# Bidirectional gated linear attention: from tiles of 66 keys to tiles of 128 keys and one of 16

## The chip, the cores and the metric

One core of a Trainium2 chip runs the whole program. The metric is the device time of one execution in microseconds (us). The core has a matmul engine (PE, with its weight loads shown as PEld), a vector engine (DVE), a scalar engine (ACT), GpSimd (POOL) and SyncE (SP), which here issues most DMAs.

## The reference

The program computes two transformer blocks one after the other on 512 tokens of width 1024. The change lies in the first block, in the mixer. 16 meta tokens stand before the 512, so there are T = 528. Of one projection it takes a differential softmax attention (4 heads) and a gated linear attention (GLA, 4 heads with 64 key and 128 value channels) that runs in both directions:

```python
def step(state, inp):                      # chunks of 64 tokens, one direction
    qc, kc, vc, gc = inp
    b = jnp.cumsum(gc, axis=2)
    rel = b[:, :, :, None, :] - b[:, :, None, :, :]
    decay = jnp.exp(jnp.where(mask, rel, -jnp.inf))
    attn = jnp.einsum('bhid,bhjd,bhijd->bhij', qc, kc, decay)
    o = jnp.einsum('bhij,bhjv->bhiv', attn, vc) + jnp.einsum('bhid,bhdv->bhiv', qc * jnp.exp(b), state)
...
    return (o_f + o_b)[:, pad:]
```

The output of the meta tokens is dropped after the mixer. After it come a router over 128x128 expert keys with 16384 small experts, and the second block (its modulation vectors come from a 1024x6144 matrix, the "ada" weights, that depends on nothing in the first block).

## The kernel before

The work is written by hand for each engine as a sequence of stages; semaphores with fixed counts join them. In the mixer the order is: norm, projections (z, gates, gla_qk, gla_v), linear attention, softmax attention, output projection.

**The linear attention has no state.** The sum of the log gates over tokens (`decay_sum`) is scanned once for each direction. Every pair (key, query) lies in one block of a binary tree over the tokens, at the level where they part. For each level and direction, a unit of work (`exponent` on POOL, `decays` on ACT and DVE) makes an array `decayed`: keys and queries times the exponential of their distance from the middle of that block. Scores of a pair are then a plain product over 64 channels, with no pair of tokens multiplied by a large number. Tokens are cut in NJ = 8 tiles of JT = 66 keys; levels have half blocks of 264, 132, 66 and 33 tokens, and leaves of 33 tokens have arrays of their own.

**Jobs and slots.** Two heads (a pair a) are done together, their 64 channels on partitions 0 to 63 and 64 to 127, their scores in PSUM banks 0 and 1. A pair has 12 jobs, each with up to 512 columns of scores of 66 keys. `scores(n)` of the PE program makes them; ACT (head 0 of the pair, first 8 jobs) and DVE (all else, and all that take a mask) copy them to SBUF as weights `residual`; `applying(n)` multiplies with the values (`gla_v`) and adds to bank 4 + h. The last four jobs hold the 66x66 blocks on the diagonal four times over: next to the leaves forward and backward and the 33-token level in both directions, each with its mask. So there are 24 slots.

**Fill.** Between `scores(n)` and `applying(n)` the PE does other work listed in `MIX_FILL[n]`: tiles of the projections gla_r, da_q, da_k, da_v (each 24 bf16 matmuls in `columns_tile` or `rows_tile`: high and low halves of an f32 product), rotations (`rope`), and "ada" blocks g = 0 to 6. An ada block (`modulation`) is 16 f32 matmul passes with 32 output rows over a 2 MB block of weights straight from its DMA stage; the next call first turns the former row (L651). Blocks 7 to 11 go with steps 0 to 4 of the softmax attention, one each, in PSUM bank 7, which they share with the sums for the head norms (L641).

**Weights** come through two f32 stage buffers (`STAGES = 2`), three high and three low ones (`SPLITS = 3`). SP loads block n once block n - 2 has left its stage: after its low half is made (`low_part` on DVE, or POOL), or, for an ada block, after its matmuls. DVE makes the low halves of da_q, da_k, da_v and of the two w_out blocks at the ends of slots 1, 5, 9, 15 and 17.

**The softmax attention** has 16 steps of 128 queries. Step n of PE: `scores(n)` (L686), `turning(n - 2)` (L696), a head sum where one is due, `applying(n - 3)` (L706), then the ada part. DVE takes maxima (L1878) and mixes (L1894), ACT takes exponentials (L1324) and copies.

## Time and profile before

| | |
|---|---|
| median of 3 runs | 2529.45 us (2520.37 to 2534.96) |
| the profiled execution | 2525.55 us |
| its span in the trace | 2524.3 us |
| PE busy | 2310.1 us (92%) |
| DVE, ACT, POOL busy | 1526.2, 908.0, 737.6 us |

The span is the time from the first to the last instruction of the profiled execution. Busy time of PE counts overlapping matmuls once; a busy PE is not a PE at its peak. Everything after the mixer (from about 553 us on) is not touched by the change.

### The profile page before, as it was taken

What the parts mean: (1) busy time and instruction counts of PE and PEld (TensorE: products, weight loads), DVE (VectorE), ACT (ScalarE), POOL (GpSimd) and SP (SyncE); (2) the same over time, 40 slices, a digit from 0 to 9 for tenths busy, and PEclk for the clock granted to TensorE, in tenths of its full rate; (3) what the DMA queues carried; (4) which work ended last, traced back from release to release, by engine and by line L of the source; (5) the groups of instructions that cost most, each with busy time, mean ns of one, the idle gap of its engine ahead of it and who ended that gap; (6) DMA issues with size and microseconds to landing.
All of it is one profiled execution on the core that took longest, in us unless ns stands there. A gap on an engine that the chain in (4) does not pass through costs nothing.

```text
span 2524.3 us, 32138 instructions
## 1 busy us (share of the span) xinstructions
PE 2310.1 (92%) x13140; PEld 1351.3 (54%) x13219; DVE 1526.2 (60%) x2530; ACT 908.0 (36%) x1074; POOL 737.6 (29%) x546
## 2 busy tenths in 40 slices
PE   6999887888979998899999999999969989899998
PEld 4567555534546554467765655555534445344443
DVE  2435426432688899999957888888856346433002
ACT  4331214422323332356643333333234155433210
POOL 4310000022042243332213333334413521355540
PEclk7999867889989999989999999999979999999999
DMA  5010544021268787677799999999922120232310
GB/s 184 34 68 34 199 149 154 1 80 72 80 254 310 243 307 248 250 275 297 296 328 361 372 379 378 381 379 373 341 94 88 67 75 13 70 105 107 133 50 33
DMA packets 194482, 483.38 MB, mean 191 GB/s; under 512 B 10677, under 2 KB 93667, under 8 KB 188320
## 3 DMA queue, kind: packets, MB, share of 16 engines
q1 hardware_dynamic: 154624, 334.65, 37.7%
q0 software_dynamic: 39712, 146.68, 15.4%
q8 instruction: 104, 1.70, 0.3%
q14 instruction: 42, 0.34, 0.0%
HBM read 428.86 MB, written 52.43 MB: 191 GB/s over the span
## 4 chain that ended last, share of the span: by engine, by line
PE 53%; DVE 24%; DMA 15%; ACT 3%; issue 3%; POOL 2%; SPq 1%; DVEq 0%; ACTq 0%; POOLq 0%
PE psum L519 12%; PE psum L518 12%; PE psum L520 12%; DMA expert_act<-act_dram 12%; DVE weight_low L1801 6%; PE psum L757 3%; DVE row_sum L2023 2%; PE psum L576 2%; PE psum L869 2%; DMA rows_b<-peer_v_dram,row_index 2%; POOL weight_low L2336 2%; PE psum L665 1%; DVE hidden_low L2189 1%; DVE norm_value L1728 1%; PE psum L742 1%
## 5 line engine op out<-in xcount | busy, mean ns | idle before, releaser
L518 PE MATMUL psum<-x_high,weight_high 128*128 128x384 bf16 (+3 forms) x1825 | 640.0, 351 | 45.5 <-DVE weight_low L1801 25.5
L519 PE MATMUL psum<-x_low,weight_high 128*128 128x384 bf16 (+3 forms) x1843 | 646.6, 351 | 24.8 <-DVE x_low L1737 16.5
L520 PE MATMUL psum<-x_high,weight_low 128*128 128x384 bf16 (+3 forms) x1843 | 646.1, 351 | 0.7
L2336 POOL TENSOR_TENSOR weight_low<-weight_stage,weight_high 128x512 bf16<-128x512 f32 (+1 forms) x237 | 312.0, 1351 | 465.6 <-ACT weight_high L1164 465.5
L1164 ACT ACTIVATE weight_high<-weight_stage 128x4096 bf16<-128x4096 f32 (+2 forms) x100 | 356.1, 3562 | 248.9 <-PE psum L520 143.2
L518 PE MATMUL psum<-hidden_high,weight_high 128*128 128x384 bf16 x1024 | 336.2, 328 | 14.5 <-DVE hidden_low L2189 14.5
L519 PE MATMUL psum<-hidden_low,weight_high 128*128 128x384 bf16 x1024 | 336.1, 328 | 0.0
L520 PE MATMUL psum<-hidden_high,weight_low 128*128 128x384 bf16 x1024 | 336.0, 328 | 0.0
L1801 DVE TENSOR_TENSOR weight_low<-weight_stage,weight_high 128x4096 bf16<-128x4096 f32 x69 | 305.6, 4430 | 36.1 <-ACT weight_high L1164 36.1
L518 PEld LDWEIGHTS psum<-x_high,weight_high 128*128 128x128 bf16 (+1 forms) x1856 | 186.0, 100 | 236.4 <-issue 40.8
L520 PEld LDWEIGHTS psum<-x_high,weight_low 128*128 128x128 bf16 (+1 forms) x1856 | 186.3, 100 | 159.0 <-issue 12.9
L519 PEld LDWEIGHTS psum<-x_low,weight_high 128*128 128x128 bf16 (+1 forms) x1856 | 186.2, 100 | 147.0 <-issue 8.8
L2426 POOL DMA_INDIRECT rows_a<-u_rows_dram,row_index x64 | 91.3, 1426 | 343.6 <-DVE rows_a L2010 254.7
L1429 ACT ACTIVATE norm_value<-psum 128x384 f32<-128x384 f32 x128 | 62.7, 491 | 344.8 <-PE psum L520 193.9
L2426 POOL DMA_INDIRECT rows_b<-peer_v_dram,row_index x64 | 108.4, 1694 | 155.5 <-DVE row_sum L2023 140.8
L2426 POOL DMA_INDIRECT rows_b<-u_rows_dram,row_index x64 | 102.6, 1603 | 160.9 <-DVE rows_b L2010 156.1
L518 PEld LDWEIGHTS psum<-hidden_high,weight_high 128*128 128x128 bf16 x1024 | 100.7, 98 | 86.2 <-issue 17.6
L520 PEld LDWEIGHTS psum<-hidden_high,weight_low 128*128 128x128 bf16 x1024 | 100.8, 98 | 67.6 <-issue 2.1
L519 PEld LDWEIGHTS psum<-hidden_low,weight_high 128*128 128x128 bf16 x1024 | 100.7, 98 | 65.3 <-issue 1.4
L2426 POOL DMA_INDIRECT rows_a<-peer_v_dram,row_index x64 | 84.5, 1321 | 156.9 <-DVE row_sum L2023 145.5
L1494 ACT ACTIVATE hidden_high<-expert_act 128x384 bf16<-128x384 f32 x128 | 61.6, 523 | 154.8 <-DVE expert_act L2185 154.8
L869 PE MATMUL psum<-gated_one_hot_b,one_hot_a 128*128 128x128 bf16 x768 | 95.8, 297 | 12.9 <-DVE gated_one_hot_b L2170 12.9
(319 smaller groups left out, 3195.1 us busy)
## 6 DMA issues: line engine op xcount, KB each, us to landing
weight_stage<-peer_u_dram SPq DMA_DIRECT2D x32, 2048.0 KB, 9.4
weight_stage<-peer_v_dram SPq DMA_DIRECT2D x32, 2048.0 KB, 11.9
weight_stage<-mlp_w_dram SPq DMA_DIRECT2D x16, 2048.0 KB, 8.2
weight_stage<-ada_w_dram SPq DMA_DIRECT2D x12, 2048.0 KB, 7.9
act_dram<-norm_value SPq DMA_DIRECT2D x128, 192.0 KB, 10.8
gate_dram<-gate_matrices SPq DMA_DIRECT2D x12, 2048.0 KB, 12.5
gates<-gate_dram SPq DMA_DIRECT2D x32, 768.0 KB, 16.8
expert_act<-act_dram SPq DMA_DIRECT2D x32, 768.0 KB, 18.4
```

Of the source, the lines that this page charges most:

```text
L518: self.nc.tensor.matmul(out, left[0], right[0], start=first, stop=False)
L519: self.nc.tensor.matmul(out, left[0], right[1], start=False, stop=False)
L520: return self.nc.tensor.matmul(out, left[1], right[0], start=False, stop=last)
L576: ins = nc.tensor.matmul(k.bank(i, hi - lo), self.m.ones[:, :], buffers.square[:, t % 4, lo:hi], start=t == 0, stop=t == KT - 1, skip_grou ...
L757: ins = nc.tensor.matmul(k.psum[:, 4 + h, i0 - META:i0 - META + ni], m.gv[:, jt, P * h:P * (h + 1)], weight[2 * (n % 2) + p][:, at:at + ni ...
L869: ins = nc.tensor.matmul(k.psum[:, i, NK * x:NK * (x + 1)], m.left[:, v, q, :, x], m.gated[part][:, v, q, :, x], start=part == 0, stop=par ...
L1164: nc.scalar.activation(k.block_view(m.w_high, n % SPLITS, n), k.block_view(m.w_stage, n % STAGES, n), ACT.Copy).then_inc(*s.w_high.up(n))
L1429: nc.scalar.activation(m.norm2.value[:, tile % 4, 0:DT], k.tile_bank(event, DT), ACT.Gelu).then_inc(*s.activated.up(*event))
L1494: nc.scalar.activation(m.hid_high[:, n % 2, b, :], m.act[:, n % 2, b, :], ACT.Copy).then_inc(*s.hid_high.up(n, b))
L1801: nc.vector.tensor_tensor(k.block_view(m.w_low, n % SPLITS, n), k.block_view(m.w_stage, n % STAGES, n), k.block_view(m.w_high, n % SPLITS, ...
L2336: ins = nc.gpsimd.tensor_tensor(m.w_low[:, n % SPLITS, at], m.w_stage[:, n % STAGES, at], m.w_high[:, n % SPLITS, at], ALU.subtract)
L2426: nc.gpsimd.indirect_dma_start(m.rows[i % ROW_SLOTS], None, v if layer else u, index).then_inc(*s.in_rows[i % ROW_SLOTS].up(i))
```

## The change

The meta tokens become a tile of 16 keys, and the other 512 keys four tiles of 128. The levels now halve blocks of 512 tokens: 256, 128, 64 and 32 tokens, with leaves of 32 (a fifth kind of unit, number 10, gives meta keys against all queries). A pair of heads has 6 jobs in place of 12: the meta tile; level 256 in each direction; level 128; the leaves of one direction (mask "same leaf and key after query"); and an inner job that holds, for each tile, the other leaves' 128x128 scores and over them, written in place in the same PSUM region, the two 64x64 and four 32x32 quadrants of levels 64 and 32. One mask and one multiplication with the values serve all three. The value tiles `gla_v` go from 8 to 5. Slots go from 24 to 12, with two fill tiles in most. Ada blocks 0 to 3 stay in slots 8 to 11; blocks 4 to 11 go with every second step of the softmax attention. The low halves of da_q, da_k, da_v, w_out 0 and w_out 1 are now made in slots 0, 2, 4, 6 and 7. POOL's exponents go from 20 to 22.

```diff
-JT = 66
-NJ = T // JT
-LEAF = JT // 2
+GLA_TILES = ((0, META),) + tuple((META + P * x, P) for x in range(QT))
+LEAF = 32
+LEVELS = (256, 128, 64, 32)
...
-    jobs = [([(t, HT, HT, 0, 0), (t + 2 * (t // 2), HT // 2 + HT * (t // 2), HT // 2, 1, 1)], None) for t in range(4)]
-    jobs += [([(4 + 2 * g + x, META, HT - META, 2, 2) for x in range(2)], None) for g in range(2)]
-    jobs += [([(2 + 4 * b + x, HT * b + (META if b == 0 else 0), HT // 2 - (META if b == 0 else 0), 3, 3)
-               for b in range(2) for x in range(2)], None)]
-    small = []
+    tile = [META + P * x for x in range(QT)]
+    own = [(1 + x, P * x, P, P * x) for x in range(QT)]
+    jobs = [(META, [(0, META, META, SEQ, 0, 0, 0, 0)], [(0, 0, SEQ, 0)], None)]
     for r in range(2):
-        for b in range(4):
-            first = JT * (2 * b + 1 - r)
-            clip = META if first == 0 else 0
-            small.append((2 * b + r, first + clip, JT - clip, 4 + r, 4 + r))
-    jobs.append((small, None))
-    for mask, (keys, queries) in enumerate(((6, 6), (7, 7), (9, 8), (11, 10))):
-        jobs.append(([(j, JT * j + (META if j == 0 else 0), JT - (META if j == 0 else 0), keys, queries)
-                      for j in range(NJ)], mask))
+        half = SEQ // 2
+        jobs.append((P, [(tile[2 * r + x], P, META + half * (1 - r), half, 1 + r, 1 + r, 0, half * x) for x in range(2)],
+                     [(1 + 2 * r + x, half * (1 - r), half, half * x) for x in range(2)], None))
+    jobs.append((P, [(tile[x], P, tile[x ^ 1], P, 3 + x % 2, 3 + x % 2, 0, P * x) for x in range(QT)],
+                 [(1 + x, P * (x ^ 1), P, P * x) for x in range(QT)], None))
+    jobs.append((P, [(tile[x], P, tile[x], P, 6, 5, 0, P * x) for x in range(QT)], own, 1))
+    inner = []
+    for x in range(QT):
+        inner.append((tile[x], P, tile[x], P, 12, 11, 0, P * x))
+        for level, array in ((2, 7), (3, 9)):
+            n = LEVELS[level]
+            for b in range(0, P, 2 * n):
+                for r in range(2):
+                    key, query = b + n * r, b + n * (1 - r)
+                    inner.append((tile[x] + key, n, tile[x] + query, n, array + r, array + r, key, P * x + query))
+    jobs.append((P, inner, own, 0))
     return jobs
...
-GLA_UNITS = (0, 2, 1, 3, 4, 5, 6, 7, 8, 9)
-GLA_JOBS = 12
+GLA_UNITS = (10, 0, 1, 2, 3, 9, 4, 5, 6, 7, 8)
+GLA_FILLS = tuple(2 if x // 2 == 4 else 1 for x in GLA_UNITS)
+GLA_ARRAYS = sum(GLA_FILLS)
+GLA_JOBS = 6
 GLA_SLOTS = 2 * GLA_JOBS
-GLA_NEEDS = (2, 2, 2, 2, 3, 3, 4, 6, 7, 8, 9, 10)
-GLA_LAST = (3, 3, 5, 6, 7, 7, 8, 9, 10, 10, 11, 11)
-GLA_FIRST = 4
-GLA_MADE = [5, 6, 7, 8, 9, 9, 9, 10, 12, 13, 14, 16, 18, 18, 18, 18, 19, 19, 19, 20, 20, 20, 20, 20]
-MIX_FILL = [[("gla_r", f)] for f in range(4)] + [[("da_q", f)] for f in range(4)]
-MIX_FILL += [[("da_k", f, 0), ("da_k", f, 1)] for f in range(4)] + [[("da_v", j)] for j in range(5)]
-MIX_FILL += [[("ada", g)] for g in range(GLA_SLOTS - len(MIX_FILL))]
-for _n, _item in ((9, ("rope_q", 0)), (9, ("rope_q", 1)), (10, ("rope_q", 2)), (10, ("rope_q", 3)),
-                  (13, ("rope_k", 0)), (13, ("rope_k", 1)), (14, ("rope_k", 2)), (14, ("rope_k", 3))):
-    MIX_FILL[_n].append(_item)
+GLA_NEEDS = (1, 2, 3, 5, 6, 11)
+GLA_LAST = (0, 1, 2, 3, 3, 4, 4, 5, 5, 5, 5, 5, 5)
+GLA_FIRST = 3
+GLA_MADE = [5, 7, 9, 11, 13, 15, 18, 20, 21, 22, 22, 22]
+MIX_FILL = [[(_name, _f), (_name, _f + 1)] for _name in ("gla_r", "da_q") for _f in (0, 2)]
+MIX_FILL += [[("da_k", _f, _g) for _f in (_x, _x + 1) for _g in range(2)] for _x in (0, 2)]
+MIX_FILL += [[("da_v", 0), ("da_v", 1)], [("da_v", 2)], [("da_v", 3), ("ada", 0)], [("da_v", 4), ("ada", 1)],
+             [("ada", 2)], [("ada", 3)]]
+for _n, _which, _h in ((4, "rope_q", 0), (5, "rope_q", 2), (7, "rope_k", 0), (8, "rope_k", 2)):
+    MIX_FILL[_n] += [(_which, _h), (_which, _h + 1)]
...
+def ada_step(n):
+    g = ADA_LATE + n // 2
+    return (g - 1, g if g < 12 else None) if n % 2 == 0 and g <= 12 else (None, None)
 
...
-            nc.tensor.wait_ge(*s.gla_decayed.at(10 * a + GLA_NEEDS[x] - 1, 1))
-            at = 0
-            for jt, i0, ni, ka, qa in k.jobs[x][0]:
+            nc.tensor.wait_ge(*s.gla_decayed.at(len(GLA_UNITS) * a + GLA_NEEDS[x] - 1, 1))
+            for j, nj, i, ni, keys, queries, row, at in k.jobs[x][1]:
                 for p in range(2):
                     rows = slice(64 * p, 64 * p + 64)
-                    ins = nc.tensor.matmul(k.psum[0:JT, p, at:at + ni], k.gla_side(a, ka)[rows, JT * jt:JT * (jt + 1)],
-                                           k.gla_side(a, qa)[rows, i0:i0 + ni], start=True, stop=True,
+                    ins = nc.tensor.matmul(k.psum[row:row + nj, p, at:at + ni], k.gla_side(a, keys)[rows, j:j + nj],
+                                           k.gla_side(a, queries)[rows, i:i + ni], start=True, stop=True,
                                            skip_group_check=True)
-                at += ni
             ins.then_inc(*s.scored.up("gla", n))
 
         def applying(n):
...
-    return p == 0 and x < 8
+    return p == 0 and x < 4
...
-            for at, name in ((1, "da_q"), (5, "da_k"), (9, "da_v"), (15, ("w_out", 0)), (17, ("w_out", 1))):
+            for at, name in ((0, "da_q"), (2, "da_k"), (4, "da_v"), (6, ("w_out", 0)), (7, ("w_out", 1))):
```

The PE program around the last jobs of the second pair, where `decayed` rows are scores, `residual,gla_v` rows apply them, L651 turns a modulation row and L665 is an ada block (one row is one or more matmuls of output rows x columns). Before:

```order
L742 MATMUL psum<-decayed_77 66x50 x2
L742 MATMUL psum<-decayed_77 66x66 x14
L651 MATMUL psum<-strip_sum,modulation_rows 128x2 x4
L665 MATMUL psum<-weight_stage,condition 32x512 x8
L757 MATMUL psum<-residual,gla_v 128x50
L757 MATMUL psum<-residual,gla_v 128x66 x7
L757 MATMUL psum<-residual,gla_v 128x50
L757 MATMUL psum<-residual,gla_v 128x66 x7
```

And now (L757 makes the scores here, L771 applies them, L667 turns, L681 is the ada block, L657 a head sum):

```order
L757 MATMUL psum<-decayed_77,decayed_78 128x128 x8
L667 MATMUL psum<-strip_sum,modulation_rows 128x2 x4
L681 MATMUL psum<-weight_stage,condition 32x512 x8
L657 MATMUL psum<-gla_square,ones 128x512
L771 MATMUL psum<-residual,gla_v 128x128 x8
L757 MATMUL psum<-decayed_75,decayed_76 128x128 x2
L757 MATMUL psum<-decayed_79 64x64 x2
L757 MATMUL psum<-decayed_80 64x64 x2
L757 MATMUL psum<-decayed_81 32x32 x2
L757 MATMUL psum<-decayed_82 32x32 x2
L757 MATMUL psum<-decayed_81 32x32 x2
L757 MATMUL psum<-decayed_82 32x32 x2
```

A job of 16 score matmuls and 16 small applying ones has become 8 and 8; the last seven rows stand four times in the inner job, once for each tile.

DVE in slot 7, between the weights of that slot and of the next (`weight_low` is the low half of w_out 1, `rope` rows rotate da_k, the RECIPROCAL belongs to the norm of head 0). Before, these pieces lay in slots 13, 14 and 17, the low half here:

```order
L1677 TENSOR_SCALAR da_v<-psum 16x512
L1933 COPY residual<-psum 66x496
L1801 TENSOR_TENSOR weight_low<-weight_stage,weight_high 128x4096
L1933 COPY residual<-psum 66x496
L1854 TENSOR_TENSOR modulation<-psum,columns 128x8
```

And now, the end of slot 7 and the start of slot 8:

```order
L1828 TENSOR_TENSOR rope_turned<-psum,rope_sin 128x264
L1830 TENSOR_TENSOR da_k<-da_k,rope_cos 128x264
L1833 TENSOR_TENSOR da_k<-da_k,rope_turned 128x264
L1812 TENSOR_TENSOR weight_low<-weight_stage,weight_high 128x4096
L1844 RECIPROCAL gla_square<-gla_square 128x512
L1943 COPY residual<-psum 128x512
```

The rotations, the low half and the reciprocal have come together ahead of the copy that slot 8 applies.

PE in the first steps of the softmax attention (L686 and L702 are scores, L696 and L712 transposes). Before, each step has an ada block:

```order
L686 MATMUL psum<-da_k,da_q 128x264 x4
L651 MATMUL psum<-strip_sum,modulation_rows 128x2 x4
L665 MATMUL psum<-weight_stage,condition 32x512 x8
L686 MATMUL psum<-da_k,da_q 128x264 x4
L641 MATMUL psum<-gla_square,ones 128x512
L651 MATMUL psum<-strip_sum,modulation_rows 128x2 x4
L665 MATMUL psum<-weight_stage,condition 32x512 x8
```

And now:

```order
L702 MATMUL psum<-da_k,da_q 128x264 x4
L667 MATMUL psum<-strip_sum,modulation_rows 128x2 x4
L681 MATMUL psum<-weight_stage,condition 32x512 x8
L702 MATMUL psum<-da_k,da_q 128x264 x4
L657 MATMUL psum<-gla_square,ones 128x512
L702 MATMUL psum<-da_k,da_q 128x264 x4
```

Step 1 has lost its turn and its block; steps 0, 2, 4 and so on to 14 have one each, and step 16 turns the last.

## Rows read from the trace of the kernel before

**Rows 1.** The page: span and busy time of PE and DVE.

```profile
span 2524.3 us, 32138 instructions
...
PE 2310.1 (92%) x13140; PEld 1351.3 (54%) x13219; DVE 1526.2 (60%) x2530; ACT 908.0 (36%) x1074; POOL 737.6 (29%) x546
```

**Rows 2.** Windows: busy time of each engine in a stretch, then granted clock and DMA.

```profile
core 0: us, PE busy (x) PEld busy (x) DVE busy (x) ACT busy (x) POOL busy (x), PEclk, DMA share, GB/s
69.50:115.90 46.40, 46.40 (x238) 25.48 (x235) 17.92 (x19) 11.46 (x15) 19.41 (x13) 1.00 0.13 46
115.90:353.40 237.50, 226.80 (x1582) 154.14 (x1593) 98.20 (x147) 60.52 (x86) 18.17 (x15) 0.87 0.31 107
290.00:353.40 63.40, 63.40 (x466) 48.12 (x463) 13.02 (x28) 8.49 (x12) 0.00 (x0) 0.63 0.60 209
353.40:483.50 130.10, 100.07 (x506) 67.39 (x508) 76.33 (x156) 61.72 (x134) 0.93 (x1) 0.75 0.28 97
```

**Rows 3.** The chain that ended last, within 115.9 to 353.4 us, by line.

```profile
by line: PE psum L757 27.0%; PE psum L520 13.0%; PE psum L518 12.9%; PE psum L519 12.8%; PE psum L742 11.3%; PE psum L665 8.2%; PE psum L651 3.4%; DMA weight_stage<-ada_w_dram 3.3%; PE psum L631 2.2%; DVE weight_low L1801 1.9%; PE psum L641
```

**Rows 4.** The same chain in order of time: start, us, what.

```profile
116.01 0.82 PE psum L742 x8
...
122.11 1.34 PE psum L757 x8
...
167.97 1.79 PE psum L757 x16
...
176.16 3.52 PE psum L757 x32
179.68 1.11 PE psum L742 x32
...
295.21 1.85 PE psum L665 x16
...
342.26 3.57 PE psum L665 x16
345.83 7.03 PE psum L757 x32
```

**Rows 5.** Waits of PE within 115.9 to 353.4 us: total, times, longest.

```profile
PE psum L665 <- DMA weight_stage<-ada_w_dram: 7.3, 1, 7.3
```

**Rows 6.** Timeline of ACT while the value tiles are made.

```profile
84.97 0.59 ACT L1175 ACTIVATE gla_v<-psum 66x512 f32<-66x512 f32 x1 [9.04 <-PE psum L520]
95.33 0.59 ACT L1175 ACTIVATE gla_v<-psum 66x512 f32<-66x512 f32 x1 [9.77 <-PE psum L520]
95.94 1.28 ACT L1280 ACT_TABLE_LOAD   x1
```

**Rows 7.** Timeline of POOL: the first two exponents.

```profile
89.90 2.08 POOL L2412 TENSOR_TENSOR decay_step<-decay_sum 128x528 f32<-128x528 f32 x2
```

**Rows 8.** Timeline of DVE in the linear attention.

```profile
241.08 0.43 DVE L1817 TENSOR_TENSOR rope_turned<-psum,rope_sin 128x264 f32<-128x264 f32 x1 [5.35 <-ACT da_v L1175]
...
246.27 3.34 DVE L1833 RECIPROCAL gla_square<-gla_square 128x512 f32<-128x512 f32 x1
...
274.55 4.41 DVE L1801 TENSOR_TENSOR weight_low<-weight_stage,weight_high 128x4096 bf16<-128x4096 f32 x1
```

**Rows 9.** Timeline of PE: a step with an ada block, then one without.

```profile
374.71 1.36 PE L686 MATMUL psum<-da_k,da_q 64*128 64x264 f32 x8
...
376.60 0.95 PE L651 MATMUL psum<-strip_sum,modulation_rows 128*128 128x2 f32 x8
381.80 3.52 PE L665 MATMUL psum<-weight_stage,condition 128*32 128x512 f32 x16 [4.24 <-DVE modulation L1854]
385.25 1.22 PE L686 MATMUL psum<-da_k,da_q 64*128 64x264 f32 x8
...
391.83 1.17 PE L686 MATMUL psum<-da_k,da_q 64*128 64x264 f32 x8
...
458.83 1.83 PE L686 MATMUL psum<-da_k,da_q 64*128 64x264 f32 x8 [0.20 <-ACT exp_scores L1324]
...
462.87 1.83 PE L686 MATMUL psum<-da_k,da_q 64*128 64x264 f32 x8 [0.20 <-ACT exp_scores L1324]
```

More of the change, by code:

```diff
@@ L370, in gla_norm_part @@
     if n < GLA_SLOTS:
-        h, part = divmod(n - GLA_JOBS, 5)
-        return (h, part) if h < 2 and part < 3 else None
+        return divmod(n - GLA_JOBS, 3)
     h, part = divmod(n - GLA_SLOTS, 3)
@@ L723, in attention @@
                 applying(n - 3)
-            if block <= 12:
-                self.modulation(block - 1, block if block < 12 else None, (7,))
-                block += 1
+            turn, block = ada_step(n)
+            if turn is not None:
+                self.modulation(turn, block, (7,))
     def linear_attention(self):
@@ L754, in applying @@
                 nc.tensor.wait_ge(*(s.act_out if gla_by_scalar(x, p) else s.dve_out).at("gla_weight", n, p))
-                at = 0
-                for jt, i0, ni, _, _ in k.jobs[x][0]:
-                    ins = nc.tensor.matmul(k.psum[:, 4 + h, i0 - META:i0 - META + ni], m.gv[:, jt, P * h:P * (h + 1)],
-                                           weight[2 * (n % 2) + p][:, at:at + ni], start=x == 0 and at == 0, stop=True,
+                n_keys, _, taken, _ = k.jobs[x]
+                for tile, i, ni, at in taken:
+                    ins = nc.tensor.matmul(k.psum[:, 4 + h, i:i + ni], m.gv[0:n_keys, tile, P * h:P * (h + 1)],
+                                           weight[2 * (n % 2) + p][0:n_keys, at:at + ni], start=x == 0, stop=True,
                                            skip_group_check=True)
-                    at += ni
                 ins.then_inc(*s.applied.up("gla", n, p))
@@ L1244, in row_tiles @@
             if name == "gla_v":
-                self.take((name, j), m.gv[:, j, :], 512, JT, ACT.Identity)
+                self.take((name, j), m.gv[:, j, :], 512, P, ACT.Identity)
             else:
@@ L1369, in attention @@
                 head(n - 3)
-            if block < 12:
+            _, block = ada_step(n)
+            if block is not None:
                 self.modulation(block)
-                block += 1
         for part in range(5):
@@ L1383, in linear_attention @@
                     nc.scalar.wait_ge(*s.applied.at("gla", n - 2, 0))
-                size = gla_columns(k, n)
-                nc.scalar.activation(weight[2 * (n % 2)][:, 0:size], k.bank(0, size, JT), ACT.Copy).then_inc(
+                n_keys = k.jobs[n % GLA_JOBS][0]
+                nc.scalar.activation(weight[2 * (n % 2)][0:n_keys, :], k.bank(0, SEQ, n_keys), ACT.Copy).then_inc(
                     *s.act_out.up("gla_weight", n, 0))
@@ L1643, in gla_sides, with gla_part @@
         sign = 1.0 if r == 0 else -1.0
[L1644 to L1660 removed]
+        return [(gla_part(i, 0, out[0]), gla_part(i, 0, q), sign), (gla_part(i, 1, out[1]), gla_part(i, 1, key), -sign)]
+    return [(gla_part(i, 0, out[0]), gla_part(i, 0, key if r == 0 else q), -1.0),
+            (gla_part(i, 1, out[0]), gla_part(i, 1, q if r == 0 else key), 1.0)]
+def gla_part(i, side, x):
+    level = GLA_UNITS[i % len(GLA_UNITS)] // 2
+    if level == 5:
+        return x[:, META:T] if side else x[:, 0:META]
+    if level == 4:
+        return x[:, META:T]
+    half = LEVELS[level]
+    return x[:, META:T].rearrange("p (b n) -> p b n", n=2 * half)[:, :, half * side:half * (side + 1)]
 def gla_weights(m):
[L1664 removed]
+    return [m.h[:, 4 + i, :] for i in range(4)]
 class VectorProgram:
@@ L1913, in attention @@
                 self.head_norm("da_head", *part)
-            if block <= 12:
-                self.modulation(block - 1)
-                block += 1
+            turn, _ = ada_step(n)
+            if turn is not None:
+                self.modulation(turn)
         for part in range(5):
@@ L1925, in scores @@
         def scores(n, p):
-            x = n % GLA_JOBS
-            mask, dst = k.jobs[x][1], weight[2 * (n % 2) + p]
+            n_keys, _, _, mask = k.jobs[n % GLA_JOBS]
+            dst = weight[2 * (n % 2) + p][0:n_keys, :]
             nc.vector.wait_ge(*s.scored.at("gla", n))
```

110 lines of the change are left out of this document (49 added, 61 removed).

## The prediction

> **What bounds the kernel now.** I read the page first: PE is busy 92% of a span of 2524.3 us, DVE 60% [rows 1]. That is an average over stages, so I cut the part that the change touches into windows [rows 2]: the value tiles (69.5 to 115.9 us, PE busy all the time), the 24 slots of linear attention (115.9 to 353.4 us, 237.5 us, PE busy 226.8, DVE 98.2, ACT 60.5), and the softmax attention (353.4 to 483.5 us, 130.1 us, PE busy 100.1). In the first two PE is the bound and the other engines have room. In the third PE idles 30 us, in a cycle of scores, maxima, exponentials and mixing. The chain inside the slots says what PE does there [rows 3]: L757 (weights times values) 27.0% and L742 (scores) 11.3%, together 38.3% of 237.5 = 91.0 us; the bf16 fill L518 to L520 38.7% = 92 us; ada blocks 8.2% and their turns 3.4% = 27.6 us; and 3.3% of waiting for an ada block's DMA. PE itself waits 7.3 us for that DMA [rows 5]. The clock is the third thing to see: granted 1.00 in the value tiles, 0.87 over the slots, 0.63 in the last 63 us, where the dense fill has given way to ada blocks and small f32 matmuls [rows 2]; the same 32 passes of L757 take 3.52 us at 176 us and 7.03 us at 346 us, and an ada block 1.85 or 3.57 us [rows 4], that is at 2.4 or at 1.2 GHz.
>
> **A. Value tiles, 8 to 5.** ACT takes every second one, at 84.97 and 95.33 us [rows 6], so one costs 10.36 / 2 = 5.18 us. A tile is 24 matmuls of 512 columns whatever its number of keys, so the tile of 16 costs the same. Three less: -15.5 us. This could uncover the chain that makes the first decays: PE would come to its first scores at 115.9 - 15.5 = 100.4 us. POOL starts the first exponents at 89.90 and has two after 2.08 us [rows 7]; the table load (1.28), two exponentials and two multiplications follow, so the meta unit is ready near 95 us. 5 us of cover are left, and I cost this at nothing.
>
> **B. Scores and values.** Prices per job at the full clock [rows 4]. Scores: 0.82 us for 396 columns of both heads, 2.07 ns a column, so 1.06 us for 512 columns. Values: 1.34 us for 396 columns, so 1.73 us for 512. For pieces of 116 to 132 columns, eight matmuls take 1.79 us, and 16 of 66 columns take 3.52: both 0.22 us each, whatever the width. So the 66-column pieces pay for their weight load, and a 128-column piece costs what a 66-column one did. That is where the change gains. New, per pair: values 3 x 1.73 + 3 x 1.79 = 10.6 us. Scores of five jobs 5 x 1.06 = 5.3 us. The inner job has 8 matmuls of 128 (1.06 us) and 48 of 64 or 32 columns, which no row shows. From above: 16 matmuls of 66 take 1.11 us, 0.069 each, so 48 take 3.3 us. From below: by columns alone, 16 x 64 and 32 x 32 at the price above, 2.1 us. Nearest is the 66-column row; I take 3.3, so the inner job is 4.4 us. A pair is 10.6 + 5.3 + 4.4 = 20.3 us, two 40.6. Slots 9 to 11 again have little dense fill; all their work at the half clock would add 11.9 us, and I take half, 6. So 46.6 against 91.0: -44.4 us (-38 to -50.5).
>
> On the quadrants the Trainium skill speaks against the change: TensorEngine Tiling (Array Packing), section Tiling Modes, says that changing the tiling mode drains the engine. The inner job changes it three times per tile, 12 times a job; with the fixed latency of 175 ns of the page TensorE: Matmul & The Clock Gate (section Single matmul latency) that is an estimate of 24 x 0.175 = 4 us, by which the sum would be 4 us less favourable. No row here shows a job with several widths of output, so the trace neither bears it out nor excludes it.
>
> **C. The late ada weights.** The DMA of ada block 1 can only start when DVE has made the low half of w_out 1, 274.55 to 278.96 us [rows 8], in the slot just before its use, hence the 7.3 us. Now that low half is in slot 7 and block 1 is used in slot 9 after a value tile, more than one slot later. -7.3 us.
>
> **D. Three ada blocks and turns leave the slots.** Seven blocks and six turns are 27.6 us there [rows 3], 2.8 + 1.35 us each: -12.4 us.
>
> **E. DVE in slot 7.** For PE that slot is 1.06 + 5.18 (one value tile of da_v) + 1.8 (rotations) + 0.9 (head sum) + 1.79 = 10.7 us. DVE has the copy (0.7), two units (1.5), a tile (0.7), 12 rotation steps of 0.43 [rows 8], low half 4.4, reciprocal 3.3: 15.8 us, all before the copy that slot 8 applies. What is late next is that copy, and the rotations of slot 8, which free PE's banks 2 and 3. The excess is 5.1 us, and slot 8 has no slack to absorb it: +5 (0 to +9).
>
> **F. Fill at the half clock.** 92 us of fill against 17 tiles of 5.2 us: about 3 us were lost to the slow clock in the masked slots. With dense tiles two by two I give back 2: -2 us.
>
> **G. The softmax attention takes eight ada blocks, not five.** A plain step takes 462.87 - 458.83 = 4.04 us; one with a block, 391.83 - 385.25 = 6.6 and 385.25 - 374.71 = 10.5 us [rows 9]. In the latter the block waits 4.24 us for DVE, because it takes bank 7 from the turn that DVE must read after its maxima and its mixing. Steps 1 and 3 lose their block; I give them back 5 us each, about a block and a turn (3.5 + 1.0) and little wait. Steps 6, 8, 10, 12 and 14 gain one: a turn (1.0 to 1.9), a wait near 0.5 and a block (3.5) are 5.2 us, almost nothing of it covered, because a plain step at this point waits only 0.20 us [rows 9]. 5 x 5.2 - 10 = +16 us. From both sides: at the 2.5 us by which the cheap step (6.6) exceeds a plain one (4.04), and 10 given back, +3; at the 6.5 us of the dear one, +22. The expensive early steps say nearer to +16. The stage buffers are no limit: each block's DMA has a step pair of at least 8 us and two buffers.
>
> DVE's fewer mask operations, ACT's 8 jobs and POOL's two more exponents lie beside PE and cost nothing: DVE is busy 98.2 of 237.5 us [rows 2] and would have about 90 of 175.
>
> **Sum.** -15.5 - 44.4 - 7.3 - 12.4 + 5 - 2 + 16 = -60.6 us. The profiled execution took 2525.55 us, 1.25 us above its span, so 2465; the median of the runs is 3.9 us higher, which would give 2469. I take 2466.
>
> **Rivals.**
> - *The ada blocks give most back.* If each of the five costs as the dear steps do, and bank 7 with DVE's later place holds the next scores (+9 each, nothing returned by steps 1 and 3), G is +45 and the total -32: 2494 us. For it: PE waited in all five blocks of the early steps. Against it: the long waits fall in steps where DVE also had 3.3 us reciprocals of the GLA norm, and such steps are now mostly without a block.
> - *The clock stays up and the waits vanish.* Slots 9 to 11 at 2.4 GHz (-6), E at 0, G at +8: -80, 2446 us. For it: fewer small matmuls between dense tiles. Against it: an ada block took 3.57 us still in the last slot [rows 4], and slots 10 and 11 hold no dense tile at all.
> - *Slower: overwriting in place serialises.* If each 64 or 32 wide matmul had to wait until the one below it was fully written, its price decides: from 60.6 / 96 = 0.63 us extra each on, nothing is gained, and from 0.76 the kernel is over 0.5% slower. The dearest small matmul in the rows is a turn, 0.95 us for four, 0.24 each, at which the sum would lose only 16 us. Little speaks for it.
> - *Nothing changes*, because PE's slots are held by DVE throughout: DVE would have to need 60 us more than PE in 12 slots, against an excess of 5 in one.
>
> **How the numbers follow.** Forecast (-50 to -70) 0.62; ada blocks dear (-30 to -50) 0.18; clock and waits better (-70 to -90) 0.15; nothing 0.025; slower 0.025. The bounds of B (12 us), E (9) and G (19) together make the forecast's own width. 2444 to 2488 us leaves out the two last cases and the outer half of the second and third, about 2 in 10. Half a per cent, 12.6 us, is what a measurement of this kernel can tell from no change: faster 0.95, same 0.03, slower 0.02.
>
> **What would show it.** A: first scores near 100.5 us, PE busy without a gap before them; a gap there says that the decays are the bound. B: jobs of 128-column pieces at 1.79 us, inner scores between 3.2 and 4.4 us; more says drain or serialisation. C: no wait of PE for ada weights. E: PE waiting a few us for DVE in slot 8. G: softmax attention about 146 us long, its even steps 9 to 10 us. The slots should end near 277 us. Wrong would be a span after the mixer that differs: nothing there is changed.

## The result and the profile after

The changed kernel takes 2420.77 us (median of 4 runs, 2418.56 to 2424.25), beside 2529.59 us for the kernel before in the same session (4 runs). The ratio is 0.9594, with a 95% interval of 0.9568 to 0.9619: 4.1% faster (the two medians alone give 0.957). The direction was forecast, the size was not: 108.8 us between the medians, and 101.3 us between the spans of the two profiled executions, where 60.6 were forecast. The time lies 23 us below the low end of the range.

The head of the page of the changed kernel, busy times as in [rows 1]:

```profile
span 2423.0 us, 31143 instructions
...
PE 2222.3 (92%) x12715; PEld 1271.7 (52%) x12715; DVE 1522.5 (63%) x2501; ACT 903.6 (37%) x1068; POOL 739.4 (31%) x548
```

PE's share is the same 92%, and its busy time fell by 87.8 of the 101.3 us (2310.1 before, [rows 1]): the kernel has become shorter mostly by time in which PE no longer works, less by waits. The windows of the same stages as [rows 2], columns: stretch, length, busy us of PE, PEld, DVE, ACT and POOL (instructions), granted clock, DMA share, GB/s. They are the slots, the softmax attention, and the last 25 us of the slots:

```profile
99.30:252.90 153.60, 150.99 (x1088) 88.85 (x1088) 94.37 (x118) 55.74 (x78) 22.98 (x17) 1.00 0.32 111
252.90:384.00 131.10, 99.34 (x580) 64.50 (x581) 76.50 (x159) 63.11 (x136) 0.93 (x1) 0.83 0.46 159
228.00:252.90 24.90, 24.90 (x276) 15.85 (x273) 10.75 (x16) 6.54 (x9) 0.00 (x0) 1.00 0.57 196
```

Set against [rows 2], the difference of 101.3 us divides so:

| stretch | before, us | after, us | measured | forecast |
|---|---|---|---|---|
| up to the first scores | 115.9 | 99.3 | -16.6 | -15.5 (A) |
| slots of the linear attention | 237.5 | 153.6 | -83.9 | -61.1 (B to F) |
| softmax attention | 130.1 | 131.1 | +1.0 | +16 (G) |
| all behind it | 2040.8 | 2039.0 | -1.8 | 0 |

The third row of the windows tells much of the miss in the slots. The last slots ran at a granted clock of 1.00, that is 2.4 GHz, where the last 63 us of the slots had 0.63 before. The chain in order of time (start, us, what) shows the same in single jobs; L757 is now the scores, L771 weights times values, L681 an ada block, L667 its turn:

```profile
99.28 1.04 PE psum L757 x4
...
110.79 1.91 PE psum L771 x4
...
235.44 1.98 PE psum L771 x16
237.42 1.09 PE psum L757 x16
238.51 0.98 PE psum L667 x8
239.50 1.85 PE psum L681 x16
241.35 1.05 PE psum L657 x2
242.41 1.78 PE psum L771 x16
244.19 3.68 PE psum L757 x100
```

The jobs of a slot without dense work (scores 1.09, turn 0.98, block 1.85, values 1.78) are 5.7 us. An ada block near the end of the slots takes 1.85 us, not the 3.57 of [rows 4]; values of 128-column pieces take 1.78 to 1.98, not the 7.03 of 66-column pieces at the half clock; and the inner job (x100) takes 3.68 us, between the bounds of 3.2 and 4.4.

PE's waits in the slots, 99.3 to 252.9 us (total, times, longest), were 7.3 us for one DMA before [rows 5]; now the three largest are

```profile
PE psum L647 <- DVE rope_turned L1828: 1.2, 2, 0.6
PE psum L757 <- DVE gla_v L1687: 0.8, 1, 0.8
PE psum L657 <- DVE rope_turned L1828: 0.6, 1, 0.6
```

and PE idles 153.6 - 151.0 = 2.6 us in all of them. In the softmax attention the largest wait, and two of its cases in the timeline of PE, are

```profile
PE psum L681 <- DVE modulation L1865: 15.0, 8, 8.1
```

```profile
274.46 3.64 PE L681 MATMUL psum<-weight_stage,condition 128*32 128x512 f32 x16 [8.12 <-DVE modulation L1865]
...
353.69 1.92 PE L681 MATMUL psum<-weight_stage,condition 128*32 128x512 f32 x16 [0.35 <-DVE modulation L1865]
```

The first row is the block of step 2, the second that of step 12; of the blocks from step 6 on only one waits more than half a us (1.72). Before, the wait was 11.1 us in 5 blocks. Of PE's waits in this stage it is the one that has grown most.

### The profile page after: what moved, and what is told of

Its sections match the earlier page's. It is cut to its first block, busy times and chain, and to the rows that moved or that the text cites. A ratio compares the mean times of both kernels' runs of the same rounds, so it can differ in the third digit from the quotient of the medians.

```text
span 2423.0 us, 31143 instructions
## 1 busy us (share of the span) xinstructions
PE 2222.3 (92%) x12715; PEld 1271.7 (52%) x12715; DVE 1522.5 (63%) x2501; ACT 903.6 (37%) x1068; POOL 739.4 (31%) x548
## 4 chain that ended last, share of the span: by engine, by line
PE 50%; DVE 26%; DMA 15%; issue 3%; ACT 3%; POOL 2%; SPq 1%; DVEq 0%; ACTq 0%; POOLq 0%
PE psum L534 13%; PE psum L535 13%; PE psum L536 13%; DMA expert_act<-act_dram 11%; DVE weight_low L1812 6%; DVE row_sum L2029 3%; DMA rows_b<-peer_v_dram,row_index 3%; PE psum L592 2%; PE psum L882 2%; POOL weight_low L2342 2%; DVE hidden_low L2195 1%; DVE norm_value L1738 1%; PE psum L681 1%; DVE expert_act L2191 1%; DVE rows_a L2016 1%
## 5 line engine op out<-in xcount | busy, mean ns | idle before, releaser
L534 PE MATMUL psum<-x_high,weight_high 128*128 128x384 bf16 (+3 forms) x1856 | 651.5, 351 | 63.1 <-DVE weight_low L1812 22.6
L536 PEld LDWEIGHTS psum<-hidden_high,weight_low 128*128 128x128 bf16 x1024 | 100.9, 99 | 67.8 <-issue 2.4
L882 PE MATMUL psum<-gated_one_hot_b,one_hot_a 128*128 128x128 bf16 x768 | 95.8, 297 | 13.9 <-DVE gated_one_hot_b L2176 13.9
```

The costliest lines, as they stand in the source:

```text
L534: self.nc.tensor.matmul(out, left[0], right[0], start=first, stop=False)
L536: return self.nc.tensor.matmul(out, left[1], right[0], start=False, stop=last)
L882: ins = nc.tensor.matmul(k.psum[:, i, NK * x:NK * (x + 1)], m.left[:, v, q, :, x], m.gated[part][:, v, q, :, x], start=part == 0, stop=par ...
```

## The experiments

There were two theories for the 23 us by which the slots are shorter than forecast: the *clock theory* (the slots are shorter because PE was granted 2.4 GHz in them all) and the *work theory* (the jobs are just cheaper). Then came the question of what had lowered the clock before. In the expectations the *wait theory* says that it was PE's wait for the ada weights, the *shape theory* that it was the narrow pieces, and the *rows theory* that it was the rows of the array that were not in use.

**1. The schedule alone.** The kernel before, with the ada blocks where the change puts them; the tiles of 66 keys stay.

```diff
-MIX_FILL += [[("ada", g)] for g in range(GLA_SLOTS - len(MIX_FILL))]
+MIX_FILL += [[] for _ in range(3)] + [[("ada", g)] for g in range(4)]
...
+def ada_step(n):
+    g = ADA_LATE + n // 2
+    return (g - 1, g if g < 12 else None) if n % 2 == 0 and g <= 12 else (None, None)
```

> The kernel before with its tiles of 66 keys, but with the new places of the ada blocks: four of them in its last four slots (slots 17 to 19 have no fill), eight with every second step of the softmax attention. By the terms C, D and G of the prediction: -7.3 - 12.4 + 16, and about 1 us of waiting in each of three empty slots, so no gain, 2526 to 2531 us. The rival, that blocks in every second step are nearly free there (the softmax attention took 131 us after the change with eight blocks, 130 us before with five) gives -7.3 - 12.4 + 1 + 3 = -16 us, 2514 us, and less still if the clock of the slots recovers too.

Measured: 2506.24 us, ratio 0.9927 (0.9889 to 0.9964), 16 us less. So about 93 of the 109 us come only with the tiles and their jobs (the interval of this run allows 9 to 28 us for the schedule). The windows of the last 53 us of the slots and of the softmax attention:

```profile
286.00:339.00 53.00, 52.31 (x414) 40.08 (x413) 12.46 (x26) 5.44 (x8) 0.00 (x0) 0.65 0.56 198
339.20:475.00 135.80, 104.21 (x578) 66.44 (x580) 76.75 (x159) 63.35 (x137) 0.93 (x1) 0.80 0.40 140
```

With no wait for an ada DMA left and fewer blocks, the clock is still 0.65 there. And eight blocks in place of five cost the softmax attention 135.8 - 130.1 = 5.7 us here, far from 16.

**2. The pieces halved again.** The changed kernel, with the values of jobs 3 to 5 in pieces of 64 columns: twice the matmuls, as in the kernel before, but 128 rows in each.

```diff
                 n_keys, _, taken, _ = k.jobs[x]
+                if x >= 3:
+                    taken = [(tile, i + lo, ni // 2, at + lo) for tile, i, ni, at in taken for lo in (0, ni // 2)]
```

> The changed kernel, with the values of jobs 3, 4 and 5 of each pair applied in pieces of 64 columns in place of 128: 48 more f32 matmuls with their weight loads, the same products. At the full clock they cost 48 x 0.22 = 10.6 us. (wait) theory: no wait is added, the clock stays at 1.00 in the slots, about 2431 us. (shape) theory: the clock falls in the slots after such jobs, above all in slots 9 to 11 beside the ada blocks, another 5 to 20 us: 2436 to 2450 us.

Measured: 2430.34 us (ratio 0.964, 0.9605 to 0.9676), 9.6 more than the changed kernel had in another session. The profiled execution was the shortest of its four (2423.17), so the slots are read for themselves:

```profile
96.20:259.80 163.60, 160.19 (x1177) 99.67 (x1185) 94.95 (x118) 55.76 (x78) 21.83 (x17) 1.00 0.31 108
```

10.0 us longer at the same clock of 1.00. Six jobs have 8 matmuls more each, 48 x 0.22 = 10.6 us. It confirms term B's rule that a piece of about 66 columns costs what one of 128 does; that the weight loads set this price is read from the equal prices and was not tested by itself. It also shows that small pieces alone, with 128 rows in use, don't bring the clock down.

**3. The inner levels left out.** The changed kernel without the scores of levels 64 and 32; the output lacks their part.

```diff
-        for level, array in ((2, 7), (3, 9)):
+        for level, array in ():
```

> The changed kernel without the 64x64 and 32x32 quadrants of the inner jobs (levels 64 and 32 are left out of the scores, 48 matmuls a pair). The inner job's scores took 3.68 us in the changed kernel; if the quadrants cost what they take there, the kernel gets 2 x 2.6 = 5 us faster, about 2415.5 us. If writing in place also drains the engine or holds DVE's copy so that more is lost around it, 10 us or more, 2411 us or less. If they are hidden, no change.

Measured: 2420.32 us (ratio 0.9595, 0.9563 to 0.9627), nothing gained. The scores took 1.09 us and not 3.68, twice, but the slots are only 0.9 us shorter (153.4 and 152.5 from the first scores to the end). The largest wait of PE (from 99 to 256 us) says why:

```profile
PE psum L534 <- DVE da_k L1687: 3.0, 1, 3.0
```

It is 0.4 us in the changed kernel. After the first inner job PE runs into DVE's copy of the da_k bank, so this job was free; only the second, in slots held by PE, is worth its 2.6 us. The first pair of heads even takes 1.7 us more (89.1 and 87.4 us), because the granted clock dips right behind that wait of 3.0 us; in the changed kernel it is 1.00 throughout:

```profile
178.00:182.00 4.00, 3.73 (x19) 2.63 (x20) 0.21 (x1) 0.00 (x0) 0.00 (x0) 0.57 0.98 370
```

I had expected that both jobs would show in the time, and missed that. The direct row stands: 48 small matmuls cost 3.68 - 1.09 = 2.6 us, 0.054 each.

**4. The late DMA.** The kernel before, the low half of w_out 1 made a slot earlier.

```diff
-            for at, name in ((1, "da_q"), (5, "da_k"), (9, "da_v"), (15, ("w_out", 0)), (17, ("w_out", 1))):
+            for at, name in ((1, "da_q"), (5, "da_k"), (9, "da_v"), (15, ("w_out", 0)), (16, ("w_out", 1))):
```

> The kernel before, with the low half of w_out block 1 made at the end of slot 16 in place of 17, so that the load of ada block 1 starts one slot earlier and PE no longer waits 7.3 us for it in slot 18. The two theories on why the granted clock was 0.63 in the last 63 us of the slots before and 1.00 after the change: (wait) it fell because of that idle time and never came back; then this kernel gains the 7.3 us and some 20 to 25 us of clock in slots 18 to 23, about 2500 us, granted clock near 1.00 there. (shape) it falls because values applied in pieces of 66 columns keep PE busy with weight loads for half the time; then it gains 7 to 8 us, about 2522 us, and the clock of the last slots stays between 0.5 and 0.75.

Measured: 2521.34 beside 2521.84 us, ratio 0.9996 (0.9979 to 1.0013). The wait only shrank:

```profile
PE psum L665 <- DMA weight_stage<-ada_w_dram: 4.3, 1, 4.3
```

so it decides nothing on whether the wait brings the clock down (the clock was 0.64 from 290 to 350 us), and its missing 3 us lie within what the interval allows. The next run takes the wait away altogether.

**5. No wait for the ada weights.** The kernel before; low halves in slots 13 and 15, the staging of w_out's high half a slot earlier too.

```diff
-            if n == 15:
+            if n == 14:
                 self.begin(("w_out", 0))
...
-            for at, name in ((1, "da_q"), (5, "da_k"), (9, "da_v"), (15, ("w_out", 0)), (17, ("w_out", 1))):
+            for at, name in ((1, "da_q"), (5, "da_k"), (9, "da_v"), (13, ("w_out", 0)), (15, ("w_out", 1))):
```

> The kernel before, with the low halves of the two w_out blocks made at the ends of slots 13 and 15 in place of 15 and 17 (the high half of w_out 1 one slot earlier too). The first try moved one low half by one slot and left 4.3 us of the wait. Now ada block 1 has its weights long before slot 18, so PE should not wait for a DMA in the slots. By the rows theory the clock still falls (0.6 to 0.7 in the last five slots) and only the wait and the warming up after it go: 7 to 9 us, ratio 0.996 to 0.997. By the wait theory the clock recovers too: 25 to 30 us, ratio 0.988 to 0.990.

Measured: 2511.13 beside 2520.08 us, ratio 0.9961 (0.9944 to 0.9977), 9 us less: term C and a little more. The slots up to the first values in pieces of 66 columns, those values, and the window of 290 to 340 us:

```profile
278.00:290.00 12.00, 12.00 (x124) 7.91 (x123) 5.58 (x6) 6.56 (x10) 0.00 (x0) 1.00 0.99 349
```

```profile
289.28 3.80 PE L757 MATMUL psum<-residual,gla_v 66*128 66x66 f32 x32
```

```profile
290.00:340.00 50.00, 50.00 (x371) 37.50 (x371) 8.28 (x25) 2.51 (x5) 0.00 (x0) 0.62 0.52 174
```

PE is busy in all of both windows. The clock is 1.00 up to the first such values and 0.62 behind them. The wait is a cost of its own; it is not what lowers the clock.

**6. Rows and pieces.** A matmul of the values before differs in two ways from one after: it has 66 rows and not 128, and 66 columns and not 128. Run 2 took the pieces; this run and the next take the rows. First the changed kernel with half pieces (run 2) and only the first 66 keys of each tile applied; the other keys are missing from the output:

```diff
-                    ins = nc.tensor.matmul(k.psum[:, 4 + h, i:i + ni], m.gv[0:n_keys, tile, P * h:P * (h + 1)],
-                                           weight[2 * (n % 2) + p][0:n_keys, at:at + ni], start=x == 0, stop=True,
+                    ins = nc.tensor.matmul(k.psum[:, 4 + h, i:i + ni], m.gv[0:min(n_keys, 66), tile, P * h:P * (h + 1)],
+                                           weight[2 * (n % 2) + p][0:min(n_keys, 66), at:at + ni], start=x == 0, stop=True,
```

> The kernel with half pieces, and in addition only the first 66 keys of each tile of 128 are multiplied with the values (the others are left out), so that the values have the shape that they had before the change: 66 rows, pieces of 64 columns, 128 columns of weights. Half pieces alone left the clock at 1.00. If rows of the array count for the clock, it falls below 1.00 in the slots as before, to some 0.6 to 0.9 in the last three, and their values take 4 to 7 us in place of 3.5. If they do not, this run is like the one with half pieces: 163 us of slots at 1.00.

Then the same edit with whole pieces:

> The changed kernel, but only the first 66 keys of each tile of 128 are multiplied with the values (the others are left out); number, width and weight loads of all matmuls stay. The full clock price of these matmuls is the same. If rows in use hold the clock up, it now falls in the slots beside the ada blocks, 3 to 15 us in all, ratio 0.961 to 0.966. If it needs half pieces as well, the slots stay at 1.00 and 153.6 us.

Measured: 2447.83 us (2 runs, ratio 0.972, 0.9668 to 0.9773) and 2422.01 us (ratio 0.9617, 0.9589 to 0.9646). The slots of the first, their last 37 us, and the slots of the second:

```profile
100.90:277.30 176.40, 172.82 (x1177) 106.54 (x1185) 95.55 (x118) 55.75 (x78) 21.82 (x17) 0.92 0.30 103
240.00:277.30 37.30, 37.30 (x344) 25.83 (x343) 12.79 (x20) 7.16 (x10) 0.00 (x0) 0.84 0.52 180
```

```profile
100.80:254.50 153.70, 151.08 (x1088) 88.92 (x1089) 94.41 (x118) 55.76 (x78) 22.98 (x17) 1.00 0.32 111
```

Half pieces with 66 rows lose 12.8 us against half pieces with 128 rows (176.4 and 163.6), at the same number of instructions; 66 rows in whole pieces lose nothing. The executions that were not profiled agree in the clock granted over the whole program: 0.945 and 0.949 for the first, 0.955 to 0.961 for the second and 0.955 to 0.960 for run 2. The chain of the first shows single jobs at the lower clock, an inner job of 5.76 and an ada block of 3.16 us:

```profile
261.68 5.76 PE psum L757 x112
...
269.24 3.16 PE psum L681 x16
```

**7. The kernel before with 128 rows.** Value tiles and weights are padded with zeros to 128 rows, and the values are applied with all 128. The zeros add nothing to the sums, and PE has the same matmuls.

```diff
-        self.gqk, self.gv = m("gla_qk", [P, 4, T]), m("gla_v", [JT, NJ, 512])
+        self.gqk, self.gv = m("gla_qk", [P, 4, T]), m("gla_v", [P, NJ, 512])
...
-    return [m.h[0:JT, 4 + i, :] for i in range(4)]
+    return [m.h[:, 4 + i, :] for i in range(4)]
...
+        nc.vector.memset(m.gv[:, :, :], 0.0).then_inc(*s.cond_cleared.up("gv"))
+        nc.vector.memset(m.h[:, 4:8, :], 0.0).then_inc(*s.cond_cleared.up("weights"))
```

> The kernel before, with rows 66 to 127 of the value tiles and of the weights set to zero once at the start (4 + 2 us of DVE beside PE) and all values applied with 128 rows in place of 66: the same products, the same number and width of matmuls, but the whole height of the array in use. If rows addressed hold the clock up, the clock of the last 63 us of the slots rises from 0.63 to near 1.00 and the kernel gains 20 to 30 us, ratio 0.988 to 0.992. If it is the arithmetic on data that are not zero, or the pieces of 66 columns, nothing changes: ratio 0.999 to 1.001.

Measured: 2501.99 beside 2520.08 us, ratio 0.9938 (0.9917 to 0.9958). The window of 290 to 340 us, in it and in the kernel before:

```profile
290.00:340.00 50.00, 48.30 (x500) 35.77 (x504) 14.73 (x36) 11.19 (x20) 0.00 (x0) 0.94 0.85 293
```

```profile
290.00:340.00 50.00, 50.00 (x402) 37.96 (x400) 11.38 (x22) 7.89 (x11) 0.00 (x0) 0.67 0.61 211
```

500 records of matmuls rather than 402 in the same 50 us. Rows of zeros, which add nothing to the result, take the granted clock from 0.67 to 0.94. In the chain the last values take 3.72 us (7.03 in [rows 4]) and a block 1.85:

```profile
330.59 1.85 PE psum L665 x16
332.44 3.72 PE psum L757 x32
```

The 0.94 still has PE's warming up behind the wait for the ada DMA (7.6 us) in it. The clean comparison starts with the first values of 66 columns behind that wait, before and in this run:

```profile
297.00:353.20 56.20, 56.20 (x390) 43.24 (x387) 8.99 (x26) 3.23 (x6) 0.00 (x0) 0.59 0.55 191
```

```profile
301.70:336.30 34.60, 34.60 (x390) 28.14 (x386) 8.66 (x26) 3.27 (x6) 0.00 (x0) 1.00 0.79 267
```

The same 390 records of matmuls take 21.6 us less. DMA traffic doesn't explain the low clock: its share is higher in this run. The whole of the slots is shorter by more than the kernel is, because setting the zeros makes the first scores late: they start at 122.5 us and not at 115.9.

```profile
122.50:336.50 214.00, 204.05 (x1593) 137.13 (x1594) 97.47 (x147) 60.53 (x86) 18.18 (x15) 0.98 0.33 113
```

214.0 us against 237.5: by this run about 23 of the 84 us that the change takes from the slots are the clock. The other 60 or so are cheaper jobs, the blocks and turns that moved out, and the wait. The executions that were not profiled agree here too: over the whole program 0.951 to 0.955 was granted, beside 0.938 to 0.947 for the kernel before.

**8. More slots without dense work.** Run 2 with the dense tiles of slots 8 and 9 moved to slot 7, so that only small matmuls and ada blocks stand in the last four slots.

```diff
-MIX_FILL += [[("da_v", 0), ("da_v", 1)], [("da_v", 2)], [("da_v", 3), ("ada", 0)], [("da_v", 4), ("ada", 1)],
+MIX_FILL += [[("da_v", 0), ("da_v", 1)], [("da_v", 2), ("da_v", 3), ("da_v", 4)], [("ada", 0)], [("ada", 1)],
```

> The kernel with half pieces, and with the last value tiles of da_v moved ahead into slot 7, so that slots 8 to 11 have no dense tile (ada blocks and rotations alone), nearer to the five such slots of the kernel before. If it is the number of such slots in a row that lets the clock fall, it falls from slot 10 on; if not, it stays at 1.00 and the time is that of half pieces, give or take a wait for the second ada block's load (up to 8 us).

Measured: 2437.46 us (2 runs, ratio 0.9679, 0.9628 to 0.973), 7 more than run 2 had in another session. The window of the slots, their last 24 us, and the largest wait of PE in them:

```profile
100.70:270.50 169.80, 163.16 (x1178) 101.17 (x1186) 94.97 (x118) 55.63 (x78) 21.83 (x17) 0.98 0.30 105
246.00:270.00 24.00, 24.00 (x290) 18.07 (x282) 8.86 (x13) 6.09 (x9) 0.00 (x0) 1.00 0.61 205
```

```profile
PE psum L647 <- DVE rope_turned L1830: 4.1, 2, 3.5
```

The slots are 6.2 us longer than in run 2, and 2.9 of this is the wait for DVE (1.2 us there). The clock was low only just behind its longest part (3.5 us), and in the light slots after that it was 1.00. That the dense fill runs out does not by itself bring the clock down to the 0.65 of before.

**9. Turn and block apart.** The changed kernel, with the turn of an ada block in an even step of the softmax attention and the next block in the odd step behind it, when DVE has read bank 7; the changed kernel ran again in the same session.

```diff
-    return (g - 1, g if g < 12 else None) if n % 2 == 0 and g <= 12 else (None, None)
+    if n % 2:
+        return None, g if g < 12 else None
+    return g - 1 if g <= 12 else None, None
...
-            if turn is not None:
+            if turn is not None or block is not None:
```

> The changed kernel with the turn of one ada block in the even steps of the softmax attention and the next block in the odd steps, in place of both in the even step. PE waited 15.0 us in all for DVE's read of bank 7 between turn and block; if that wait is on the path, some 10 us go, about 2410 us. If it only stands for the later wait for maxima and exponentials, which then takes its place, 0 to 4 us. Rival: the odd steps hold the head sums (1, 7, 11, 15) in the same bank, and the block then waits for those: no gain or a few us slower.

> The changed kernel once more, as the base of this call on this chip: ratio 0.959, about 2420 us; slots 153.6 us long at a granted clock of 1.00.

Measured: 2404.16 us (ratio 0.954, interval 0.9496 to 0.9583) beside 2418.26 for the changed kernel again (0.9601, 0.9562 to 0.9641). The softmax attention:

```profile
253.50:370.60 117.10, 98.95 (x578) 66.34 (x579) 76.78 (x159) 63.05 (x137) 0.93 (x1) 0.83 0.50 176
```

14.0 us shorter than 131.1 with the same work, and no block waits for DVE's modulation. This is the fastest version of all.

## Why the prediction was right in kind and wrong in size

The spans differ by 101.3 us where 60.6 were forecast. Of these 41 us, 23 lie in the slots, 15 in the softmax attention, 1 ahead of the slots and 2 behind the attention. Three steps failed: work of the last slots and blocks was priced at the lower clock (B, D, G), DVE's excess in slot 7 was put on PE's path (E), and the gained blocks were taken as not covered (G). For the slots, PE's time by its timeline (from each row's start to the next, waits apart), in us:

| | before | after | measured | forecast |
|---|---|---|---|---|
| scores and values | 95.8 | 40.5 | -55.3 | -44.4 (B) |
| ada blocks and turns | 30.4 | 10.4 | -20.0 | -12.4 (D) |
| fill | 90.5 | 89.6 | -0.9 | -2 (F) |
| rotations, head sums | 10.7 | 10.2 | -0.4 | 0 |
| PE idle | 10.3 | 2.9 | -7.5 | -7.3 + 5 (C, E) |

**A held.** First scores at 99.3 us against 100.4 forecast, -16.6 against -15.5. PE waited 0.8 us for DVE's last value tile, not for the decays, so the cover of 5 us was enough. The difference of 1 us means nothing: with the same work ahead of them, the first scores of the changed kernel run again and of its versions in runs 2, 3, 6, 8 and 9 start between 96.2 and 100.9 us.

**B's working held, its clock did not.** At the full clock it gave 40.6 us for all scores and values, and they took 40.5. The step that failed is "I take half, 6": the work of the last slots was not slowed at all. The other 4.8 us are in the base: by line, the chain gave 91.0 us, but where it runs over DVE and the late DMA it leaves out what PE did beside them, and the timeline has 95.8. On the quadrants run 3 and the row of 3.68 us speak: by the full-clock prices of rows the job was to take 3.2 to 4.4 us, and no drain beyond that shows. The Trainium skill, TensorEngine Tiling (Array Packing), section Tiling Modes, says that a change of mode drains the engine; the prediction's estimate of 4 us from the latency is for both inner jobs, so a job would have taken some 2 us more, 5.3 to 6.5 us. The measurement decides: 3.68 us leaves at most 0.5 us over the lower bound, and at these sizes the drain isn't seen.

**C held.** The wait is gone, and PE's idle time in the slots fell from 10.7 to 2.6 us. Run 5 shows it alone, at 9 us.

**D was too small for the same reason as B.** I took a mean block (2.8 us) and turn (1.35) of before and left four blocks and three turns at that price, 15.2 us. They took 4 x 1.85 + 3 x 0.98 = 10.3. And the base was low here too, 27.6 us by the chain and 30.4 by the timeline. Measured -20.0 against -12.4.

**E failed.** "slot 8 has no slack to absorb it: +5" is wrong: in slot 8 PE does not wait for the weights that this copy makes. The timeline of DVE:

```profile
212.24 4.42 DVE L1812 TENSOR_TENSOR weight_low<-weight_stage,weight_high 128x4096 bf16<-128x4096 f32 x1
216.58 3.35 DVE L1844 RECIPROCAL gla_square<-gla_square 128x512 f32<-128x512 f32 x1
219.84 0.63 DVE L1943 COPY residual<-psum 128x512 f32<-128x512 f32 x1
```

DVE is as late as forecast, but PE needs this copy only when it applies slot 8, at 224.51 us, 4 us after it is there (219.84 + 0.63): the slot's own scores, tile and block lie between. I counted DVE's excess over a slot and not the distance to the instruction that needs it.

**F** gave -0.9 against -2. Rotations and head sums, which I had left out, are the same in both kernels (-0.4). So the excess over the forecast in the slots is 10.9 us (B), 7.6 (D) and 5 (E), less 1.1 (F).

**G was the largest single error:** +16 forecast, +1.0 measured. "A block (3.5)" failed: of the five steps that gain a block, four have it at 1.92 us and one at 2.96, 10.6 us together and not 17.5. This explains 7 of the 15 us. "Almost nothing of it covered" failed too. The windows of steps 0 to 5 and of the rest, in the kernel before, then in the changed one:

```profile
353.23:410.48 57.25, 39.77 (x231) 21.57 (x231) 28.19 (x60) 24.39 (x50) 0.00 (x0) 0.78 0.48 168
410.48:483.50 73.02, 60.47 (x276) 45.99 (x278) 48.14 (x97) 37.33 (x85) 0.93 (x1) 0.73 0.12 42
```

```profile
252.86:301.77 48.91, 31.97 (x177) 17.72 (x176) 27.78 (x58) 23.18 (x48) 0.00 (x0) 0.76 0.43 151
301.77:384.00 82.23, 67.41 (x405) 46.83 (x406) 48.72 (x102) 39.92 (x89) 0.93 (x1) 0.87 0.47 164
```

The first six steps gave back 8.3 us (10 forecast). The rest grew by 9.2 us and not by 26, though its turns and blocks took 17.0 us of PE and their waits 3.3: the scores, transposes and values there, the same matmuls in both kernels, took 49.3 us and not 58.6, at a granted clock of 0.87 where it was 0.73. In the schedule-alone run the whole stage grew by 5.7 at a clock of 0.80. Why the clock of this stage is higher with more blocks in it is not settled by a run. The waits for DVE's modulation grew by 3.9 us (11.1 to 15.0), and run 9 shows what the choice of the same step for turn and block costs: 14 us.

**The rival that won** is "the clock stays up and the waits vanish", to which I gave 0.15. Even its numbers (-6, E at 0, G at +8) reach only -80, and what was measured, 101 to 109 us, lies beyond every range that I had given a chance. I kept its chance low because an ada block took 3.57 us in the last slot of before; that row was taken as a sign of what blocks without dense work do. Runs 2, 6 and 7 show that the values around it did this: in the changed kernel, while PE was busy, the clock fell only with 66 rows and pieces of half the width together.

**What stays open.** What about 66 rows in pieces of 66 columns the clock answers to isn't told apart further; run 7 says only that rows of zeros do as well as rows of data, and the scores, which have 64 rows in both kernels, were not varied. Behind waits of 3 us and more the clock dips too (runs 3 and 8), but those dips are short. The spans differ by 101 us and the medians by 109, because the profiled execution of the kernel before was 4 us faster than its median and that of the changed kernel 3.5 us slower than its own. The kernel before varies by some 15 us between runs (2520.37 to 2534.96 here, a median of 2514.46 in another session), and the 1.8 us behind the attention lie within that.

## What to carry to other kernels

Before splitting an f32 matmul into pieces narrower than 128 columns, count its weight loads: pieces of 50 to 132 columns cost 0.22 us each at the full clock, so the widest tile wins, and overwriting small squares in place over it (0.054 us each) is cheap. When a change widens such matmuls, price what stays around them at both clocks and give the upper one a real chance, because the granted clock may go with the shape of the small work and not with the amount of dense work. And an engine that runs late costs only from the first instruction that needs it: measure the distance to that one before putting a sum on the excess.

## What was not expected of the hardware

- Zero rows raise the clock: the same program with the values' matmuls padded from 66 to 128 rows was granted 0.94 and not 0.67 in the stretch of 290 to 340 us, and took 18 us less (2501.99 beside 2520.08). From the first values of 66 columns behind the wait on, the same 390 records took 34.6 us at 1.00 and not 56.2 at 0.59. A matmul's time did not depend on its rows otherwise: whole pieces with 66 or 128 rows gave slots of 153.7 and 153.6 us.
- Neither half-width pieces (1.00) nor 66 rows (1.00) lowered the clock of the slots alone; together they did (0.92, and 0.84 in the last 37 us). PE was busy in all of that stretch, and so it was in run 5's 50 us at 0.62: the clock fell with no idle time before it there.
